# First mixer of a two-block transformer kernel: heads between the steps of QKV and of the output projection, reversed bias rows, four sums on GpSimd

## The reference, cut to what matters

```python
def first_block(x, c, ada_w, ada_b, norm_mix, norm_ffn, ffn_w1, ffn_w2, a_w_in, ...):
    cond = jax.nn.silu(c)
    for i in range(DEPTH):
        m, j = i % N_MIXERS, i // N_MIXERS
        mod = cond @ ada_w[i] + ada_b[i]
        sh1, sc1, g1, sh2, sc2, g2 = [t[:, None, :] for t in jnp.split(mod, 6, axis=-1)]
        h = rms_norm(x, norm_mix[i]) * (1.0 + sc1) + sh1
        if m == 0:
            y = chunked_relpos_attention(h, a_w_in[j], a_q_gain[j], a_k_gain[j], a_rel_bias[j], a_w_out[j])
        elif m == 1:
            y = chunked_spatial_gating(h, b_w_in[j], b_v_gain[j], b_w_s[j], b_b_s[j], b_w_out[j])
...
        x = x + g1 * y
        h = rms_norm(x, norm_ffn[i]) * (1.0 + sc2) + sh2
        x = x + g2 * squared_relu_mlp(h, ffn_w1[i], ffn_w2[i])
    return x
```

## Time and profile before

| | us |
|---|---|
| median of 3 runs | 1184.97 (1182.8 to 1185.09) |
| the profiled execution | 1183.74 |
| its span, first to last instruction | 1182.1 |
| PE busy | 1135.7 (96%) |
| DVE busy | 768.6 (65%) |
| ACT busy | 528.4 (45%) |
| POOL busy | 94.7 (8%) |

### The profile page before, as it was taken

One profiled execution on the slowest core, in us unless ns is written; L12 is line 12 of the kernel. 1 busy time (PEld: TensorE's weight loads), 2 busy tenths in 40 slices (PEclk: granted clock), 3 DMA queues, 4 the chain that ended last, 5 costly groups with the idle time before them and its releaser, 6 DMA issues.

```text
span 1182.1 us, 18513 instructions
## 1 busy us (share of the span) xinstructions
PE 1135.7 (96%) x6212; PEld 965.7 (82%) x6212; DVE 768.6 (65%) x1322; ACT 528.4 (45%) x865; POOL 94.7 (8%) x138
## 2 busy tenths in 40 slices
PE   6999799999999999999999999999999999899997
PEld 6777698798998968889997899899788677688675
DVE  5688647588788477787868546545683572773662
ACT  1445541354454356544443435434455441654441
POOL 1042000100000010100000000000020020110020
PEclk8799557899999989999999899999899999899999
DMA  9878525287877548766774455653465200566001
GB/s 372 319 280 295 170 90 204 72 287 274 302 265 271 190 155 302 271 215 213 248 242 161 136 180 163 215 190 116 144 221 188 79 12 19 170 215 204 25 0 44
DMA packets 60135, 222.27 MB, mean 188 GB/s; under 512 B 6548, under 2 KB 14484, under 8 KB 53944
## 3 DMA queue, kind: packets, MB, share of 16 engines
q1 hardware_dynamic: 48176, 168.97, 41.5%
q0 software_dynamic: 5760, 41.95, 9.9%
q10 hardware_dynamic: 6152, 10.77, 2.8%
HBM read 220.61 MB, written 4.20 MB: 190 GB/s over the span
## 4 chain that ended last, share of the span: by engine, by line
PE 79%; issue 8%; DVE 6%; POOL 3%; DMA 2%; ACT 1%; DVEq 0%; SPq 0%; POOLq 0%; ACTq 0%
PE ps L1347 21%; PE ps L1348 21%; PE ps L1349 21%; DVE w_lo L831 2%; POOL rinv L412 2%; PE ps L1519 2%; PE ps L1442 2%; PE ps L1701 1%; PE ps L1432 1%; PE ps L1414 1%; PE ps L1396 1%; PE ps L1699 1%; PE ps L1739 1%; DMA raw<-in_wstream 1%; PE ps L1508 1%
## 5 line engine op out<-in xcount | busy, mean ns | idle before, releaser
L831 DVE TENSOR_TENSOR w_lo<-raw,w_hi 128x1024 fp32r<-128x1024 f32 (+1 forms) x318 | 357.0, 1168 | 116.6 <-ACT w_hi L507 111.6
L507 ACT ACTIVATE w_hi<-raw 128x1024 fp32r<-128x1024 f32 (+1 forms) x318 | 307.8, 1009 | 194.5 <-DMA raw<-in_wstream 110.4
L1347 PE MATMUL ps<-w_hi,h_hi 128*128 128x512 f32 (+1 forms) x512 | 204.0, 398 | 3.4 <-DVE h_lo L912 3.4
L1347 PE MATMUL ps<-h_hi,w_hi 128*128 128x256 f32 x704 | 202.6, 288 | 0.7 <-DVE h_lo L912 0.5
L1348 PE MATMUL ps<-w_lo,h_hi 128*128 128x512 f32 (+1 forms) x512 | 201.4, 393 | 0.0
L1349 PE MATMUL ps<-h_hi,w_lo 128*128 128x256 f32 x704 | 200.9, 285 | 0.0
L1348 PE MATMUL ps<-h_lo,w_hi 128*128 128x256 f32 x704 | 200.9, 285 | 0.0
L1349 PE MATMUL ps<-w_hi,h_lo 128*128 128x512 f32 (+1 forms) x512 | 200.9, 392 | 0.0
L1347 PEld LDWEIGHTS ps<-h_hi,w_hi 128*128 128x128 f32 x704 | 137.0, 195 | 3.8 <-issue 2.2
L1347 PE MATMUL ps<-w_hi,a_hi 128*128 128x512 f32 x352 | 137.4, 390 | 0.7 <-DVE a_lo L1172 0.7
L1348 PEld LDWEIGHTS ps<-h_lo,w_hi 128*128 128x128 f32 x704 | 136.9, 195 | 0.7
(11 more groups left out here) (163 smaller groups left out, 1328.7 us busy)
## 6 DMA issues: line engine op xcount, KB each, us to landing
raw<-in_wstream SPq DMA_DIRECT2D x296, 512.0 KB, 5.5
ada_raw<-in_adastream POOLq DMA_DIRECT2D x40, 1024.0 KB, 5.1
ada_raw<-in_adastream SPq DMA_DIRECT2D x4, 1024.0 KB, 9.1
arena<-in_adastream SPq DMA_DIRECT2D x4, 1024.0 KB, 10.7
rel_rows<-in_relrev ACTq DMA_DIRECT2D x1, 3072.0 KB, 20.8
raw<-in_wsmall SPq DMA_DIRECT2D x22, 128.0 KB, 2.1
row<-in_gate_rows ACTq DMA_DIRECT2D x5, 512.0 KB, 3.7
row<-in_params ACTq DMA_DIRECT2D x2, 769.0 KB, 4.0
```

Source lines behind the costliest of these rows:

```text
L507: act.activation(w_hi[:, c % SPLIT, at], raw[:, n, 0:width // 2], ACT.Copy)\
L831: nc.vector.tensor_tensor(w_lo[:, c % SPLIT, at], raw[:, (2 * c + h) % RAW, 0:width // 2], w_hi[:, c % SPLIT, at].bitcast(F32), ALU.subtract)\
L1347: nc.tensor.matmul(dst, sh, mh, start=start, stop=False)
```

## The change

1. SP loads the chunks of the first mixer in the order q, k, v of the first eight heads, then q, k, v of the other eight (FIRST_CHUNKS). Three passes run before the heads. Passes 3 to 5 and the output projection are cut into steps of one token tile (`qkv_step`, `out_step`), and one stands ahead of each head on PE; in heads 6 to 8 two steps and transposes of units. The projection goes by pairs of 128 features as each four heads are done.
2. q is transposed in reversed order of the positions (`backward` reads the PSUM tile backwards), and so are the outputs. With that the bias can be read from its own 16 rows with ascending partitions: the 3 MB copy goes, two bias loads move from ACT to SP, behind chunk 1.
3. Scores and the product with v of a head three turns earlier share a bank, 4 or 5 (HEAD_BANK); the probabilities' transposes go to banks 6 and 7. Each head is divided by its sums by itself (`normalise`).
4. GpSimd does the ada sums 11, 13, 15 and 17 (`pool_sum`), each a multiply of 2048 elements and three adds of 1024, 512 and 256. DVE does 8, 9, 10, 12, 14, 16, 18, 19.
5. `columns` moves behind the projection, with `modulation` behind the residual; the last ACT and DVE steps are ordered anew; 14 warm-up matmuls in place of 20.

```diff
-WARM = (20, 16, 16, 16)
+WARM = (14, 16, 16, 16)
+FIRST_CHUNKS = (0, 1, 4, 5, 8, 9, 2, 3, 6, 7, 10, 11, 12, 14, 13, 15)
+HEAD_BANK = (4, 5, 4, 5, 4, 5, 5, 5, 5, 4, 5, 4, 4, 5, 4, 5, 5, 4, 5)
+UNIT_BANK = {0: 4, 1: 5, 4: 6, 5: 7, 2: 4, 3: 4, 6: 5, 7: 4}
+POOL_ADA = (11, 13, 15, 17)
...
-            src = bass.AP(rel_rows.tensor, heads * REL + P,
-                          [[HEADS * REL - 1, P], [REL, 4], [1, S]])
+            src = bass.AP(relrev_in.tensor, heads * 512 + 1, [[1, P], [512, 4], [1, S]])
...
+            def pool_sum(a):
+                n = POOL_ADA.index(a)
+                pool.wait_ge(s_araw[1], 16 * (a // 2 - 3))
+                v = ada_raw[:, 1]
+                own.inc(nc.gpsimd.tensor_tensor(v, v, cond[:].unsqueeze(2)
+                                                .to_broadcast([P, KT, AW]), ALU.mult))
+                for m in (4, 2):
+                    own.wait()
+                    own.inc(nc.gpsimd.tensor_tensor(v[:, 0:m], v[:, 0:m], v[:, m:2 * m], ALU.add))
+                own.wait()
+                nc.gpsimd.tensor_tensor(ada_acc[:, (a + ADA_AT) % ADA_KEPT, :], v[:, 0], v[:, 1],
+                                        ALU.add).then_inc(s_pool_ada, 1)
+                pool.wait_ge(s_pool_ada, n + 1)
+                pool.dma_start(ada_raw[:, 1].rearrange("p a b -> p (a b)"), adastream[a + 2])\
+                    .then_inc(s_araw[1], 16)
...
+            ada_load(adastream[12], 0, 11)
+            pool_sum(11)
+            ada_load(adastream[14], 0, 12)
+            head_rinv(2)
+            pool_sum(13)
+            head_rinv(3)
+            ada_load(adastream[16], 0, 13)
+            pool_sum(15)
+            pool_sum(17)
+            ada_load(adastream[18], 0, 14)
+            ada(20, 2)
```

DVE, before the heads and in them:

```diff
+            split(3)
+            q_sums(0)
+            split(4)
+            q_heads(0)
+            split(5)
+            ada_part(8, 8)
+            split(6)
+            q_sums(1)
+            split(7)
+            q_heads(1)
+            ada_part(9, 9)
+            unit_lo(0)
+            unit_lo(1)
+            split(8)
             dve.wait_ge(s_bias, 32)
             mask(row[:, 0:D])
             mask(gate[:])
+            ada_part(10, 10)
+            unit_lo(4)
+            unit_lo(5)
...
+                if h >= 3:
+                    normalise(h - 3)
+                if h < HEADS:
+                    a, q = 12 + 2 * (h // 4), h % 4
+                    if h == 12:
+                        dve.wait_ge(s_pool_ada, len(POOL_ADA))
+                        dve.sem_inc(s_ada, len(POOL_ADA))
...
+                    marks = ada_part(a, (11, 12, 13, 18)[h // 4], range(2 * q, 2 * q + 2), marks)
+                if 1 <= h <= 5:
+                    lo_part(9 + (h - 1) // 2, (h - 1) % 2, CW)
+                if h == 4:
+                    q_sums(2)
+                if h == 5:
+                    q_heads(2)
+                    lo_part(11, 1, CW)
+                    unit_lo(2)
+                if h == 6:
+                    lo_part(12, 0, CW)
+                    lo_part(12, 1, CW)
+                    q_sums(3)
+                    lo_part(13, 0, CW)
+                    unit_lo(3)
                 if h == 7:
+                    q_heads(3)
+                    lo_part(13, 1, CW)
+                    out_lo(0)
                     dve.wait_ge(s_late[0], 16)
                     mask(row[:, 0:D])
+                    lo_part(14, 0, CW)
+                    unit_lo(6)
+                    lo_part(14, 1, CW)
+                    unit_lo(7)
```

PE, the turns of the heads:

```diff
+            for h in range(HEADS + 3):
+                if h < 6:
+                    if h == 3:
+                        pe.wait_ge(s_v, 2)
+                    qkv_step(3 + h // 4, h // 2 % 2, h % 2)
+                if h == 6:
+                    qkv_step(4, 1, 0)
+                    pe.wait_ge(s_norm, 2)
+                    transpose_qk(2)
+                    qkv_step(4, 1, 1)
+                if h == 7:
+                    pe.wait_ge(s_tok, 6)
+                    qkv_step(5, 0, 0)
+                    pe.wait_ge(s_qklo, UNIT_AT[2] + 1)
+                    transpose_qk(3)
+                    qkv_step(5, 0, 1)
+                if h == 8:
+                    pe.wait_ge(s_qklo, UNIT_AT[3] + 1)
+                    transpose_out(0)
+                    qkv_step(5, 1, 0)
+                    pe.wait_ge(s_norm, 5)
+                    transpose_qk(6)
+                    qkv_step(5, 1, 1)
+                    pe.wait_ge(s_h, 5)
+                    transpose_qk(7)
+                if 10 <= h <= 13:
...
+                    out_step(0, (h - 10) // 2, h % 2)
+                if h == 12:
+                    pe.wait_ge(s_norm, 8)
+                    transpose_out(1)
+                if 14 <= h <= 17:
+                    out_step(1, (h - 14) // 2, h % 2)
+                if h == 16:
+                    pe.wait_ge(s_norm, 12)
+                    transpose_out(2)
+                if h == 18:
+                    out_step(2, 0, 0)
+                bank_read(h)
...
+            out_step(2, 0, 1)
+            pe.wait_ge(s_norm, 16)
+            transpose_out(3)
+            out_step(2, 1, 0)
+            out_step(2, 1, 1)
+            pe.wait_ge(s_pTc, 16)
+            pe.wait_ge(s_ada, 18)
+            gate_sum(8, (6, 7))
+            for t in range(TT):
+                for cb in range(2):
+                    out_step(3, cb, t)
             pe.wait_ge(s_ada, 20)
-            columns(12, 6)
+            columns(12, 5)
```

More of the change, by code:

```diff
@@ L1019, in _, with ada_part, q_sums @@
-            split(C_WO + 3)
+            def ada_part(a, count, tiles=range(KT), marks=()):
+                if tiles[0] == 0:
+                    dve.wait_ge(s_araw[a % 2], 16 * (a // 2 - 3))
+                return ada_sum(ada_raw[:, a % 2], ada_acc[:, (a + ADA_AT) % ADA_KEPT, :], count,
+                               tiles, marks)
+            def q_sums(q):
+                for t in range(TT):
+                    dve.wait_ge(s_qsq, 2 * q + t + 1)
+                    head_sums(tok[q % 2][:, t, :], ss8[:, t])
@@ new lines, in qkv_step @@
+            def qkv_step(p, half, t):
+                c = 2 * p + half
+                if t == 0:
+                    chunk_in(c)
+                for n in range(4):
+                    k = 4 * half + n
+                    if p == 0 and t == 0:
+                        operand_in(0, k)
+                    last = matmul3(ps[:, (p % 2) * 2 + t, :], tokens(k, t), weights(c, 512, n),
+                                   k == 0, k == KT - 1)
+                if half == 1 and t == 0:
+                    last.then_inc(s_half, 1)
+                if t == 1:
+                    last.then_inc(s_used, 1)
@@ L1482, in head_parts @@
+            for p in range(3):
+                if p == 2:
+                    pe.wait_ge(s_tok, 2)
+                for half in range(2):
+                    for t in range(TT):
+                        qkv_step(p, half, t)
+                if p == 1:
+                    pe.wait_ge(s_h, 4)
+                    transpose_qk(0)
+                    transpose_qk(1)
+            transpose_qk(4)
+            transpose_qk(5)
             def head_parts(h, a, b, c, d):
```

409 lines of the change are left out of this document (232 added, 177 removed).

## The result

The changed kernel takes 1176.09 us (median of 14 runs, 1169.93 to 1181.28), the kernel before 1185.64 us, timed beside it (14 runs, 1179.33 to 1189.42): a ratio of 0.9913, 95% interval 0.9895 to 0.9932. It is faster by 0.9%, 9.6 us, a little less than half of the 20 us that the forecast gave (1165 against 1184.97). The profiled execution took 1173.97 us, its span 1172.3 us, against 1183.74 and 1182.1.

A forecast was written before the change was run, and what follows sets the result against it. PE and DVE bound QKV together; PE then stood empty and ran the heads at half clock. PE's 165 us plus waits and clock gave E = 192.4, MLP at 208.4, 18.4 us less: 1165 us, own range 1157 to 1173, wide 1146 to 1189.

The forecast's parts named there:

- PE's 165: First mixer: PE alone, at full clock and without waits, would finish the output projection at 165 us, against 215.7.
- a head at full clock: PE's work on one head: estimated at 1.8 us, half of the 3.59 us at half clock.
- end of pass 0 and start: QKV's beginning: pass 0 ends at about 52.2 us, unchanged from the kernel before.
- wait 1: Ahead of head 0: PE stands 4.4 us for DVE's unit 4 of K, then half clock costs some 2.5.
- wait 2, with sum 13: Unit 2 in head 6: scaling 3.5 us behind PE, 2 of clock; GpSimd's sum 13 adds 2.
- heads 8 and 9: Sum 15 delays DVE's splits and units 6 and 7: 16 us with clock through head 11, counted as 12.
- head 12 (sum 17): GpSimd's sum 17 is done before DVE asks for all four at head 12: no more than 1 us.
- end of the projection: First mixer's output projection, called E: ends at 192.4 us, PE's 165 plus the waits and their clock.
- A: Rival, heads: GpSimd and DVE hardly meet, so DVE keeps up; 13 us more gain, 1152 (1144 to 1157); chance 0.22.
- B: Rival, heads: clock returns late, or GpSimd's chain holds DVE at head 12; half the remaining gain goes, 1173 to 1182; 0.12.
- C: Rival: clock stays at the lower level from head 8's hole to the heads' end; slower, 1189; chance 0.16.
- the contention term: DVE's splits and ada tiles beside GpSimd's sums: 0.75 of shared time lost, bounds nothing or 0.85 of 33 us.

The follow-up runs named there:

- e_bias: Changed kernel with its first two bias loads moved from behind chunk 1 to behind the fourth chunk loaded; 1180.58 us, ratio 0.9959 to the kernel before.
- e_gap: Changed kernel with VectorE's sums of chunks 12, 14, 16, 18 squeezed into fewer heads and chunk 18's load asked for earlier; 1166.13 us, ratio 0.9846 to before.
- e_nosum: Changed kernel with GpSimd's four sums cut to their last addition (result not the reference's); 1160.01 us, ratio 0.9800 to the kernel before.
- e_low: Changed kernel with VectorE's low parts of units 4 and 5 put ahead of chunk 8's split and chunk 10's sum; 1174.55 us, ratio 0.9924 to before.
- e_no15: Changed kernel with only GpSimd's sum of chunk 15 cut to its last addition (result not the reference's); 1169.75 us, ratio 0.9891 to the kernel before.
- e_gaplow: e_gap with VectorE's low parts of units 4 and 5 early as well; 1169.29 us, ratio 0.9887 to the kernel before.

## Why the prediction was right in direction and wrong in size

The direction held, and so did the mechanisms of the holes; the time lies in the wide range (1146 to 1189), but outside the forecast's own (1157 to 1173), and the gain is a little less than half of what was forecast. What failed is the first term of the sum, "PE's 165": it took the start as unchanged and a head at full clock as 1.8 us. By the forecast's steps, in the profiled executions:

| step | forecast | measured |
|---|---|---|
| end of pass 0 and start | unchanged | first QKV matmul 42.93, 3.4 us late |
| wait 1 | 4.4 + 2.5 clock | 4.6 + about 2.5 |
| wait 2, with sum 13 | 5.5 + 2 | 3.7 + about 1.7 |
| heads 8 and 9 | 12, about half of it clock | 5.0 + about 5.5 |
| head 12 (sum 17) | at most 1 | 1.8 + about 1.7 |
| a head at full clock | 1.8 (estimate) | 2.02 |
| end of the projection | 192.4 | 200.1 |
| from there to the MLP | 16 | 16.2 |

(The clock parts are half of the busy time spent at 0.50 in the windows.) The waits, the hardest part of the sum, came to 26.5 us against 27.4. Single ones were off both ways (head 12, "no more than 1 us", came to 3.5), and that they cancel is luck. The two terms behind "PE's 165" failed.

**The start.** "Unchanged" was wrong for this execution by 3.4 us. The change's loads don't decide it: kernels with them at the old place and at the new one show both starts. It is a difference between executions, and the trace of before showed one side of it. Whether the kernel before has the late start too no trace shows; some of its runs have the same sign, a longer time at a higher recorded clock (beside e_bias, 1184.6 to 1187.1 us at 0.941 to 0.945, against 1182.0 to 1183.9 at 0.933). So how much of the miss in the medians is the start stays open.

**The price of a head at full clock.** I halved the 3.59 us of the earlier trace rows. In the changed kernel the three transposes of a head start at these times, with one QKV step of 2.72 us in each round:

```profile
98.65 0.55 PE L1757 MATMUL ps<-ident,both 128*128 128x128 f32 x3
98.95 0.48 PE L1493 MATMUL ps<-w_hi,h_hi 128*128 128x512 f32 x1
...
101.81 0.78 PE L1738 MATMUL ps<-arena,both 128*128 128x64 f32 x6
...
103.39 0.55 PE L1757 MATMUL ps<-ident,both 128*128 128x128 f32 x3
```

4.74 - 2.72 = 2.02 us. Of the 0.22 us above the estimate, 0.14 lies in the QKV step: it takes 2.86 us (98.95 to 101.81) between small matmuls, where a dense run gives 2.72. The head's own part is 1.88, near half of 3.59; the price of putting the two together was missing. Over 16 heads 0.22 is 3.5 us (an estimate; a round with a step of the projection, 173.31 to 176.66 us, gives 3.35 - 1.36 = 1.99). With the start's 3.4 it makes 6.9 of the 7.7 us by which the projection ended late; the rest I can't place. Behind it another 0.2 us lie between the projection and the MLP, and 0.8 behind that, which the forecast had as unchanged and where the MLP now begins at the lower clock.

**What the sum left out though it came out in the total.** The chunk loads were mentioned for VectorE once ("requested only when sum 10 is done") and never priced, and they were 10.8 us of DVE's time, though the longest of the three waits cost PE only 0.45 us. That PE's waits nevertheless add up is partly luck: the contention term was set near the top of its bounds (0.75 lost; the longest split beside a sum, 1.2 us of work in 4.5, lost 0.73, but the average of 15 splits is only 0.57 us over), and as a share of speed it had the wrong form: the rows show turns, so the loss goes by how long the GpSimd instruction still runs. That it filled the room of the missing term is my reading. e_gap, which takes the waits for loads away and moves tiles, is 7.5 us of mixer shorter, e_nosum, without the sums' work, 11.1.

**The rivals.** A (GpSimd and DVE hardly meet) is refuted by the 4.53 us split and by e_nosum. B gave the measured time, 1173 to 1182, but only part of its mechanism: the clock did come back, after 3 to 5 us of work at heads 0, 6 and 12 and 11 us behind heads 8 and 9; the POOL chain with its loads in one line did hold DVE at head 12, for 6.3 us, but PE hardly (0.45 us). C, the clock staying low to the end, is refuted: in the changed kernel it is at 1.00 again from 160 us. What I should have asked is not what the sums on GpSimd cost beside DVE, but whether they pay at all: 13.4 us of VectorE's time saved, against 8.5 us lost on the splits (26.8 - 15 x 1.22) and 5.0 on the tiles of its own sums, as much again as was saved, and the sums' 38 us in the queue that also issues the loads.

## To carry to other kernels

When work is moved to an engine that shares memory interfaces with the bound engine, price all three: the work saved there, the slowing of what runs beside it, and the delay of everything that the receiving engine's queue also does, DMA issue above all; here the sum was against the move, and undoing it, which also made the loads earlier, gave 1.1%. A load that is asked for only when the buffer's last reader is done needs its latency as slack in the reader's order: squeezing that reader's work, at no work less, gave 0.7%. In these runs closing one pause didn't give its length: e_low, e_no15 and e_gaplow each closed one and found the next, so fix what several pauses share first, and only then the order.

## What the runs showed of the hardware

**The recorded clock can stand at 1.00 while PE runs at the lower rate.** The start differs by 3 us between executions of nearly the same code: the first QKV matmul comes at 39.6 to 40.1 us in eight of the fourteen profiles, at 42.8 to 43.2 in six. In all of them PE multiplies single columns from 20 to 21.6 us on. The kernel before, then the changed one, in the same window of 1 us, and then PE's rows:

```profile
22.00:23.00 1.00, 1.00 (x12) 1.00 (x11) 1.00 (x3) 0.00 (x0) 0.00 (x0) 1.00 1.00 418
...
22.00:23.00 1.00, 1.00 (x6) 1.00 (x6) 1.00 (x4) 0.00 (x0) 0.00 (x0) 1.00 0.98 410
```

```profile
8.92 6.96 PE L1442 MATMUL ps<-cond,arena 128*128 128x1 f32 x32 [8.92 <-DMA arena<-in_adastream]
15.74 3.65 PE L1396 MATMUL ps<-ident,arena 128*128 128x128 f32 x16
...
20.61 11.25 PE L1442 MATMUL ps<-cond,arena 128*128 128x1 f32 x64
...
9.20 6.96 PE L1588 MATMUL ps<-cond,arena 128*128 128x1 f32 x32 [9.20 <-DMA arena<-in_adastream]
...
21.40 13.81 PE L1588 MATMUL ps<-cond,arena 128*128 128x1 f32 x64
```

12 products reach into this us there, 6 here, with 1.00 in both records. The rows before it show what this is. The first 32 products take 6.95 or 6.96 us in all fourteen profiles, 4.6 a us, the rate of the changed kernel's later 64 (13.81 us). The 16 transposes behind them take 3.65 us in both of these kernels, as much as 16 at a recorded 0.50 do (3.67 at 210.88 us, above). So in both PE begins at the lower rate, though the record says 1.00. The early kind speeds up between 18 and 21 us, without a step in the record, and keeps it until the record falls to 0.50 (near 23.5 us in the kernel before); then 6 products reach into each us there too. The late kind doesn't speed up there: its first QKV matmuls take 0.63 us each until 48 us, as the early kind's do at a recorded 0.50, and its own record stays at 1.00 all that time. I read this as a record that shows 1.00 until the first change that it catches; what decides between the kinds was not shown. For the reader it means that a rate of matmuls is the better witness, and that the mean clock can be higher in the slower execution: the changed kernel's four runs with a mean clock of 0.947 to 0.950 took 1169.9 to 1173.0 us, the ten with 0.952 to 0.960 took 1171.9 to 1181.3.

**Contention works both ways.** GpSimd's last addition of a sum, 128x256, takes 0.73 to 0.75 us in sums 11 and 13 and 1.59 in sum 15, where a split runs beside it, and the four sums take 8.2, 9.1, 10.8 and 9.9 us where the forecast had 8.3 for each. That is the smaller part: 2.5 us more for the longest, against the 3.3 us that one split beside it lost. In sum 15 the turns can be followed to the end: the multiply ends at 141.26 us, the split beside it at 142.35; the first addition at 144.56, the next split at 145.65; the second addition at 146.77, the third split at 147.85; the last addition at 148.44. Each split ends 1.08 or 1.09 us behind a GpSimd instruction, whenever it began, and the same holds for the long splits of e_gap and e_gaplow (3.51, 4.40, 3.89 and 4.19 us). So what a split loses is what is left of the GpSimd instruction that it meets. GpSimd's small roots (128x8) don't hold one: 1.21 us at 132.12, beside a root that began at 131.97. That shorter GpSimd instructions would cost VectorE less at each meeting follows from this, but no run tried it.
